# A hybrid encoder layer on one core: mLSTM scores and turned keys made once per chunk, exponent rows by DMA, query scaled ahead of its product, gates kept raw

## The reference

```
def step(carry, xs):                        # one chunk, one direction, one head
    C, n, m = carry
    qc, kc, vc, li, lf = xs
    b = cumsum(lf)
    d = b[..., :, None] - b[..., None, :] + li[..., None, :]     # lower triangle only
    m_inter = b + m
    m_t = max(m_inter, max(d))
    w_inter = exp(m_inter - m_t)
    a = (qc @ kc.T) * exp(d - m_t)
    num = w_inter * (qc @ C) + a @ vc
    den = w_inter * (qc @ n) + sum(a)
    h = num / max(|den|, exp(-m_t))
    wk = exp(g - m_new) * kc
    C_new = decay * C + wk.T @ vc ;  n_new = decay * n + sum(wk)
...
h = sigmoid(mo) * (h_fwd + h_bwd) ;  h = h * rsqrt(mean(h*h) + eps) * norm_w
merged = sigmoid(g_att) * (ya @ w_att) + sigmoid(g_mlstm) * (ym @ w_mlstm)
```

## Time and profile before

| | us |
|---|---|
| median of three runs | 2833.33 |
| span of the profiled execution | 2828.1 |
| profiled execution's own time | not listed apart; the runs lie 5.0 to 6.3 above the span |
| prologue, to the first mLSTM phase | 194.3 |
| mLSTM phase of head 1, to the turn of its values | 168.9 |
| rest of head 1 | 168.5 |
| everything behind the last attention phase | about 1243 |
| busy: PE, DVE, POOL, ACT | 2598.7, 1794.3, 1051.1, 635.4 |

### The profile page before, as it was taken

How to read it: one execution, slowest core, us unless ns; L and a number is a source line. 1 busy time by engine, 2 the same in 40 slices (tenths; PEclk the granted TensorE clock), 3 DMA queues, 4 the chain that set the end, 5 groups by cost and what they waited for, 6 DMA issues and landing times.

```text
span 2828.1 us, 40134 instructions
## 1 busy us (share of the span) xinstructions
PE 2598.7 (92%) x15036; PEld 2372.0 (84%) x15036; DVE 1794.3 (63%) x2582; ACT 635.4 (22%) x1445; POOL 1051.1 (37%) x490
## 2 busy tenths in 40 slices
PE   7799999999899989999588899898999999999996
PEld 4688778787787877788477799898999999999996
DVE  5537766687667766677767564878875126876312
ACT  4101343223431233313422101231210111111001
POOL 4511220213202221021412235565566665666663
PEclk9899999999999999999789999999999999999998
DMA  3101210112111211112242443231323233232321
GB/s 111 59 30 55 81 41 27 41 52 85 29 32 40 74 64 31 28 47 72 103 140 80 146 130 117 90 112 67 122 86 112 101 102 141 74 111 74 112 83 60
DMA packets 106845, 223.51 MB, mean 79 GB/s; under 512 B 9720, under 2 KB 52232, under 8 KB 106688
## 3 DMA queue, kind: packets, MB, share of 16 engines
q1 hardware_dynamic: 78016, 203.08, 21.0%
q10 hardware_dynamic: 28672, 18.36, 2.5%
HBM read 173.91 MB, written 47.42 MB: 78 GB/s over the span
## 4 chain that ended last, share of the span: by engine, by line
PE 72%; DVE 15%; DVEq 4%; ACT 3%; issue 3%; DMA 1%; ACTq 0%; POOL 0%; POOLq 0%; SPq 0%
PE ps L1637 18%; PE ps L1639 18%; PE ps L1638 18%; PE ps L1813 3%; PE ps L1670 2%; PE ps L1672 2%; PE ps L1671 2%; PE ps L1832 2%; DVE prob L1350 2%; DVEq L1293 1%; PE ps L1735 1%; DVE o_ld L1292 1%; PE ps L1750 1%; DVE small L1328 1%; DVE prob L1325 1%
## 5 line engine op out<-in xcount | busy, mean ns | idle before, releaser
L669 POOL TENSOR_TENSOR ring_h<-raw,colt 128x1024 fp32r<-128x1024 f32 x229 | 444.9, 1943 | 1665.3 <-PE ps L1639 948.3
L672 POOL TENSOR_TENSOR ring_l<-raw,ring_h 128x1024 fp32r<-128x1024 f32 x229 | 565.5, 2469 | 32.5
L1637 PE MATMUL ps<-ht_h,ring_h 128*128 128x512 f32 (+3 forms) x1464 | 536.1, 366 | 26.9 <-DVE ht_l L1424 9.3
L1638 PE MATMUL ps<-ht_l,ring_h 128*128 128x512 f32 (+3 forms) x1464 | 521.7, 356 | 0.0
L1639 PE MATMUL ps<-ht_h,ring_l 128*128 128x512 f32 (+3 forms) x1464 | 521.3, 356 | 0.0
L1637 PE MATMUL ps<-h_h,ring_h 128*128 128x320 f32 (+1 forms) x1408 | 440.4, 313 | 19.6 <-DVE f_z L1550 11.5
L1638 PE MATMUL ps<-h_l,ring_h 128*128 128x320 f32 (+1 forms) x1408 | 439.4, 312 | 0.0
L1639 PE MATMUL ps<-h_h,ring_l 128*128 128x320 f32 (+1 forms) x1408 | 439.2, 312 | 0.0
L1637 PEld LDWEIGHTS ps<-ht_h,ring_h 128*128 128x128 f32 x1464 | 278.6, 190 | 67.0 <-DVE ht_l L1424 10.2
L1486 DVE TENSOR_TENSOR acc<-acc,sq 128x322 f32<-128x322 f32 (+1 forms) x84 | 113.5, 1351 | 312.1 <-ACT sq L740 310.3
L1639 PEld LDWEIGHTS ps<-ht_h,ring_l 128*128 128x128 f32 x1464 | 277.9, 190 | 35.9
(11 more groups left out here) (231 smaller groups left out, 4680.1 us busy)
## 6 DMA issues: line engine op xcount, KB each, us to landing
raw<-w SPq DMA_DIRECT2D x229, 512.0 KB, 3.3
gate_scratch<-g_st SPq DMA_DIRECT2D x32, 256.0 KB, 2.0
xr<-xt SPq DMA_DIRECT2D x2, 2568.0 KB, 9.7
x_scratch<-x SPq DMA_DIRECT2D x2, 2568.0 KB, 8.6
zo_scratch<-o_st SPq DMA_DIRECT2D x40, 128.0 KB, 1.7
o_ld<-zo_scratch ACTq DMA_DIRECT2D x40, 128.0 KB, 2.1
ym_scratch<-y_st ACTq DMA_DIRECT2D x40, 128.0 KB, 1.9
ya_scratch<-ya_st ACTq DMA_DIRECT2D x40, 128.0 KB, 2.5
```

Source lines behind the costliest of these rows:

```text
L669: nc.gpsimd.tensor_tensor(ring_h[:, :, slot * P:(slot + 1) * P], raw[:, rslot], one_col.unsqueeze(2).to_broadcast([P, KT, P]), ALU.mult)
L672: nc.gpsimd.tensor_tensor(ring_l[:, :, slot * P:(slot + 1) * P], raw[:, rslot], ring_h[:, :, slot * P:(slot + 1) * P].bitcast(F32), ALU.su ...
L1637: mm(out_ap, wh, hi(k + k_first), start=first and k == 0, stop=False)
L1638: mm(out_ap, wh, lo(k + k_first), start=False, stop=False)
```

## The change

Scores and turned keys are made once per chunk, in five steps instead of ten, and ACT keeps both (the turned keys over the keys themselves). The matmuls with `pick` are gone: the exponent's row and the row of inter-chunk factors are loaded broadcast over the partitions by DMAs of ACT's queue (`load_rows`, two a step), POOL adds the mask (`mask_rows`), ACT makes the exponential with the other part as bias. POOL scales the query by its factor ahead of the product with the state (`scale_queries`, one buffer `qw`), so that both halves of the numerator add up in one bank, and it scales the keys (`scale_keys`). The two directions' updates use the same two banks, one after the other. Gates are stored raw, and their sigmoid is 0.5 (1 + tanh(z/2)), with the tanh on ACT ahead of the gate products in the last attention phase and in the mixing. Four dense groups of the mLSTM phase move: step 8 has one group, step 9 one, and three stand behind it.

On SP and POOL, and the table of dense groups:

```diff
+A_STEP = [[1]] + [[2 * i, 2 * i + 1] for i in range(1, 8)] + [[16], [17]]
...
-                    sp.wait_ge(s_g1, lin(lambda hh: 12 * hh + pos + 1, h))
+                    sp.wait_ge(ev_act, lin(lambda hh: GROUPS[("A", hh, pos)][3], h))
...
+            def mask_rows(i, h, shift=0):
+                pool.wait_ge(m_bw[i % 2], lin(lambda k: 32 * (5 * (k + shift) + i // 2 + 1), h))
+                nc.gpsimd.tensor_tensor(bw[:, i % 2, :, 0], bw[:, i % 2, :, 0], mask[:], ALU.add).then_inc(m_um, 1)
+            def scale_queries(i, h):
+                if i > 1:
+                    pool.wait_ge(m_nd, lin(lambda k: NB * k + i, h))
+                for d in range(2):
+                    if not fresh(d, i):
...
+                        last = nc.gpsimd.tensor_tensor(qw[:, d], mq_t[:, :, c * P:(c + 1) * P],
+                                                       bw[:, i % 2, d, 1].unsqueeze(1).to_broadcast([P, 2, P]),
+                                                       ALU.mult)
+                last.then_inc(m_q, 1)
+            def mlstm(h):
+                take(lambda k: a_unit(k, 0), h)
+                pool.wait_ge(m_sel, lin(lambda k: k + 1, h))
+                scale_keys(0, h)
+                take(lambda k: a_unit(k, 1), h)
+                for i in range(NB - 1):
+                    scale_queries(i + 1, h)
+                    if i + 1 < NB - 1:
+                        scale_keys(i + 1, h)
+                    if i + 2 < NB:
+                        mask_rows(i + 2, h)
+                    if i + 2 < A_UNITS:
+                        take(lambda k, u=i + 2: a_unit(k, u), h)
+            for i in range(2):
+                mask_rows(i, 0)
             with pool.Fori(0, HEADS - 1) as h:
-                for u in range(A_UNITS):
-                    take(lambda k, u=u: a_unit(k, u), h)
+                mlstm(h)
```

On ACT, the mLSTM phase:

```diff
             def mlstm(h, dense):
+                exponents(0, h)
+                keep_scores(0, h)
+                evac_a(0, h)
                 for i in range(NB):
-                    act.wait_ge(m_e, lin(lambda k: NB * k + i + 1, h))
-                    nc.scalar.activation(ex[:], ex[:], ACT.Exp).then_inc(m_x, 1)
-                    if i >= 5:
...
+                    if i + 1 < NB:
+                        exponents(i + 1, h)
+                    if i > 5:
+                        finish_y(i - 1, h)
+                    evac_a(A_STEP[i][0], h)
+                    if i + 2 < NB:
+                        load_rows(i + 2, h)
+                    if i + 1 < NB // 2:
+                        keep_scores(i + 1, h)
+                    if i >= 5:
+                        output_gate(i, h)
+                    for g in A_STEP[i][1:]:
+                        evac_a(g, h)
```

On DVE, the mLSTM phase:

```diff
+                weights(0, h)
                 for i in range(NB):
+                    normalise_h(i, h)
+                    state(0, i, h)
                     if i >= 5:
+                        gated(i, h)
+                    state(1, i, h)
                     if i + 1 < NB:
+                        weights(i + 1, h)
```

On PE, the numerator and the order of the phase, and on DVE the product with a gate:

```diff
             def m_numden(i, h):
...
+                    pe.wait_ge(m_q, lin(lambda k: 9 * k + i, h))
+                    pe.wait_ge(m_h, lin(lambda k: NB * k + i, h))
                 for d in range(2):
                     if not fresh(d, i):
+                        pe.wait_ge(m_c[d], lin(lambda k: 8 * k + updates_to(d, i - 1), h))
                         for dt in range(2):
-                            mm(ps[:, 3 + 2 * d, 0:DH + 1], mq_t[:, dt, c * P:(c + 1) * P], c_st[:, d, dt],
+                            mm(ps[:, 3 + d, 0:DH + 1], qw[:, d, dt], c_st[:, d, dt], start=dt == 0, stop=False)
...
             def mlstm(h, is_dense):
+                m_scores(0, h)
+                unit_group("A", 0, 0, h)
                 for i in range(NB):
-                    m_scores(i, h)
-                    unit_group("A", (2 * i) // 3, (2 * i) % 3, h)
                     m_numden(i, h)
+                    m_update(0, i, h)
                     if i > 5:
                         m_turn(i - 1, h)
-                    unit_group("A", (2 * i + 1) // 3, (2 * i + 1) % 3, h)
-                    m_update(i, h)
-                unit_group("A", 6, 2, h)
+                    unit_group("A", A_STEP[i][0] // 3, A_STEP[i][0] % 3, h)
+                    m_update(1, i, h)
+                    if i + 1 < NB // 2:
+                        m_scores(i + 1, h)
+                    for g in A_STEP[i][1:]:
+                        unit_group("A", g // 3, g % 3, h)
+                for g in range(18, 21):
+                    unit_group("A", g // 3, g % 3, h)
...
-                V.tensor_tensor(gw[:, a:b], gw[:, a:b], ps[:, n % 2, 0:b - a], ALU.mult).then_inc(b_mix, 1)
+                V.scalar_tensor_tensor(gw[:, a:b], gw[:, a:b], 1.0, ps[:, n % 2, 0:b - a], ALU.add, ALU.mult
+                                       ).then_inc(b_mix, 1)
```

More of the change, by code:

```diff
@@ L438, in updates, with updates_to, side @@
         return i + 1 < NB and not fresh(d, i + 1)
+    def updates_to(d, i):
+        return sum(updates(d, n) for n in range(i + 1))
+    def side(d, i):
+        return int(chunk_of(d, i) >= NB // 2)
     def tcol(q, d, h, c):
@@ L702, in _ @@
+            mlstm(HEADS - 1)
             for n in range(U_B, U_B + 2):
@@ L943, in evac_a, with exponents @@
                          rows=slice(HD, P)).then_inc(ev_act, 1)
+            def exponents(i, h):
+                act.wait_ge(m_um, lin(lambda k: NB * k + i + 1, h))
+                if i >= 2:
+                    act.wait_ge(m_nd, lin(lambda k: NB * k + i - 1, h))
+                for d in range(2):
+                    last = nc.scalar.activation(ex[i % 2][:, side(d, i)], bw[:, i % 2, d, 0], ACT.Exp,
+                                                bias=tcol(0, d, h, chunk_of(d, i)))
+                last.then_inc(m_x, 1)
@@ L1095, in attend @@
                             evac_m(g, h, 1)
+                    if not dense and j >= 1:
+                        gate_tanh(2 * j - 2)
+                        gate_tanh(2 * j - 1)
+                    if dense and j == NB - 1:
+                        act.wait_ge(a_s_done, lin(lambda k: NB * (k + 1), h))
+                        for i in range(2):
+                            load_rows(i, h, 1)
                     evac_o(j, h)
@@ L1099, in attend @@
                 store_o(NB - 1, h)
+                if not dense:
+                    for n in range(2 * NB - 2, 3 * KT):
+                        gate_tanh(n)
                 for s in range(2):
@@ new lines, in state @@
+            def state(d, i, h):
+                if not updates(d, i):
+                    return
+                dve.wait_ge(m_cu[d], lin(lambda k: 8 * k + updates_to(d, i), h))
+                src = ps[:, 5:7, 0:DH + 1]
+                if fresh(d, i):
+                    last = V.tensor_copy(c_st[:, d], src)
+                else:
+                    last = V.scalar_tensor_tensor(
+                        c_st[:, d], c_st[:, d], decay[:, bass.ds(h * NB + (d * HEADS * NB + chunk_of(d, i)), 1)], src,
+                        ALU.mult, ALU.add)
+                last.then_inc(m_c[d], 1)
@@ new lines, in normalise_h, with gated @@
+                last.then_inc(m_h, 1)
+            def gated(i, h):
+                ch = [chunk_of(d, i) for d in range(2)]
+                dve.wait_ge(m_ze, lin(lambda k: 5 * k + i - 4, h))
+                V.reciprocal(o_ld[:], o_ld[:])
+                dve.drain()
+                for d in range(2):
+                    V.tensor_tensor(h_acc[:, ch[d]], h_acc[:, ch[d]], o_ld[:, d], ALU.mult)
+                dve.drain()
+                for d in range(2):
+                    last = V.scalar_tensor_tensor(o_ld[:, d], h_acc[:, ch[d]], 1.0, h_acc[:, ch[d]],
+                                                  ALU.mult, ALU.mult, accum_out=small[:, 6 + d:7 + d])
+                last.then_inc(m_ss, 1)
@@ L1246, in mlstm @@
                     next_columns(h + 1)
+                weights(0, h)
                 for i in range(NB):
-                    step = lambda k, i=i: NB * k + i + 1
-                    ch = [chunk_of(d, i) for d in range(2)]
-                    dve.wait_ge(m_sc, lin(step, h))
-                    for d in range(2):
-                        last = V.scalar_tensor_tensor(ex[:, d], ps[:, 2, 256 * d + P:256 * d + 2 * P],
-                                                      tcol(0, d, h, ch[d]), mask[:, d], ALU.add, ALU.add)
```

274 lines of the change are left out of this document (128 added, 146 removed).

## The result

The changed kernel takes 2923.18 us (median of 4 runs, 2922.41 to 2924.74), the kernel before 2833.86 beside it: ratio 1.0317, 95% interval 1.0302 to 1.0332. It is 89 us slower, where 57 were forecast, and the median lies 1.2 us above the upper end of the range. The profiled execution took 2922.41 us, its span is 2920.6, so 92.5 above the span before. In these four runs the time lies 1.8 us above the span; by that the profile before belongs to an execution of about 2829.9 us (my estimate), 3 us under its median, and this is why the spans differ by 92.5 and the medians by 89.

The account below looks back on a forecast made before the run. PE was taken as the bound of the mLSTM phase. Per head -11.1 - 6.8 + 24.8 + 6.0 = +12.9 us; four heads +51.6, with head 0's start +57, so 2833.3 becomes 2890 us; range 2842 to 2922.

Parts of the forecast that it names:

- POOL's queue: Before step 6, PE waits for POOL's scaled query behind unit 6's split, which waits for its load: +10.4 us a head.
- The output gate's chain: Steps 6 to 8: ACT's output gate stands behind the first group's copy, so PE waits +1.9, +2.0 and +6.5 us.
- The gain on PE: mLSTM phase: ten steps of 16 passes become five of 12, at 0.111 us a pass: -11.1 us a head.
- POOL's pair of products: POOL's two query products before PE's numerator, priced from its split rows at 1.2 us with an issue between them.
- The start of head 0: POOL masks head 0's first rows before splitting unit 0, 7.5 us later with some 2 covered: +5, bounds 3 and 8.
- The other heads' starts: Row loads go out a dense group (5.5 us) earlier and unit 0 has some 5 us to spare: 0.
- Unit 5's wait: Unit 5 waits for group 8, first of step 4; the 10.4 us chain is partly covered by update and group: +4.0.
- The clock: PE runs at half clock behind the waits of 4.0, 10.4 and 6.5 us: +6.0 us a head, bounds 0 and 7.8.
- Gates: DVE's sigmoid work ends under PE's cover and the tanh moves to ACT: 0, bounds -2 and +8.
- A: POOL's queue does not hold PE, as unit loads land before step 5's end: +1.0 us a head, 2842; chance 0.10.
- B: PE stays the bound all through, as DVE is relieved in steps 5 to 9: -67 us, 2767; chance 0.06.
- C: Contention: POOL's small instructions hold each DVE chain 2 us in steps 5 to 9, 10 a head: 2930; chance 0.07.

Follow-up runs that it names:

- late_takes: Changed kernel with POOL splitting units 5 and 6 later, behind the scaled queries of steps 5 and 7: 2875.53 us, ratio 1.0146.
- the kernel start: Changed kernel with POOL splitting a head's unit 0 ahead of masking its first two row pairs: 2900.76 us, ratio 1.0239.
- the kernel three: Changed kernel with units 5 and 6 split later, ACT's output gate at the step's head and unit 0 split ahead of the first masks: 2785.58 us, ratio 0.9839.

## Why the prediction was right and where it failed

The direction and the two mechanisms were right: with POOL's queue, the output gate and the first masks put back in order, 135 us went. **POOL's queue** in front of step 6 was forecast at 10.4 us and is 11.26. **The output gate's chain** was forecast at 1.9, 2.0 and 6.5 and is 1.26, 2.09 and 6.03; the 4.5 that was to lie under unit 6's wait came up as 4.18 in late_takes. **The gain on PE** of 11.1 us a head is 8 to 10 by the doubled scores, so this term was taken 1 to 3 us a head too high. The estimate for POOL's pair of products, 1.2 us, measured 1.40; here the splits' rows were the right scale. By the GPSIMD Engine Reference (introduction) of the Trainium skill, with its factor of two, the pair would take 1.9 us (an estimate); the trace's 1.40 does not bear that out.

Span against span, the loss is 35.5 us more than forecast. The steps that failed are the starts of the heads, the landing of unit 5, and a part of the clock:

**The start of head 0, +5.** Measured: +3.8 in the prologue, and of the 28.7 of its phase 11.7 more than head 1's. The step priced the row loads and the masks (7.5 us) and took off 2 of cover, which leaves 5.5, but left out that unit 0's split stands behind them. Before the change it ran 192.16 to 196.55, beside the prologue's end. Now it follows the masks:

```profile
206.66 0.72 POOL L712 TENSOR_TENSOR bw<-bw,mask 128x256 f32<-128x256 f32 x1 [0.91 <-DMA bw<-rows_scratch]
207.34 1.89 POOL L682 TENSOR_TENSOR ring_h<-raw,colt 128x1024 fp32r<-128x1024 f32 x1
209.38 2.34 POOL L685 TENSOR_TENSOR ring_l<-raw,ring_h 128x1024 fp32r<-128x1024 f32 x1
```

PE's last score ended at 199.65. The masks ended 7.7 us behind it (207.38), where 5.5 were forecast, and the split 4.3 later: 12.1 of the 12.20 measured. The 3.8 in the prologue stay in the kernel start, and no run took them apart. I had counted what POOL's new instructions cost, and not what the old one behind them loses in cover.

**The other heads' starts, 0.** Right for heads 1 and 2, where PE has some 6.5 us of its own at the loop's end, and wrong for head 3, which is written out behind the loop and has 1.70: there the first masks ran at 1274.29 and 1276.84 and the split behind them cost 7.23 and its clock. I read one head's start and took it for all. Of the 22 us that the edit of POOL's first masks gave back, 20 lie in these two heads, against 5 forecast. With the prologue's 3.8, this one step is about half of the 35.5.

**Unit 5's wait, +4.0.** The chain was right and the landing was not: 6.85 us from issue to split in place of 3.56, as the row loads that the change adds ran beside it. The wait was 7.52, and 4.35 with them moved: 3.2 us in head 1, and 14 us over the four heads. The prediction counted the new DMAs as issues on ACT, not as traffic.

**The clock, +6.0 a head.** Head 1's account closes with 6.7 if the passes are taken at 11.1; the granted clock gives 8.7 - 1.6 = 7.1, and the fill of two waits gave 6 back. So the size was nearly right. The reading that failed is that a wait of 2.12 us leaves the clock at 1.00: of step 8's, 2.09 us long, 1.2 us were lost in head 1, and in other heads and kernels the same wait cost nothing.

**Gates, 0.** The last attention phase and mixing got 4.2 us shorter, more than the bound of -2. That was not taken apart by a run.

Of the rivals, A fell with 7.52 and 11.26 us on POOL's query, and B with 30 us of idle PE. C did not explain the changed kernel: DVE's pairs of output gate products take 0.76 to 0.82 us in all its steps and heads. But its mechanism is real. It comes up once the queues are mended: in the kernel three it is 3.4 of the 5.18 us before step 9, the largest loss left there, and in the kernel with unit 6 split last it took that wait from 6.04 to 11.59.

## What to carry to other kernels

When a critical instruction is put into the queue of an engine that waits for loads, price it at the end of the longest chain ahead of it, and price the old work behind it too: three changes of order in two queues, with no work changed, were worth 135 us and turned 3% slower into 1.6% faster. A head that is written out behind a loop starts without the loop's slack, so look at it by itself. Removing one wait lays bare the next, so the gain of a set of edits can't be added up from each alone: here it was 135 against 100.

## What the runs showed of the hardware

Idle PE costs more than its idle time: behind each wait of 7.5 and 11.3 us some 2.3 us of work were lost to the 1.2 GHz level, and filling the idle time with products that nobody reads made the kernel 25 us faster. A wait of 2.1 us cost 1.2 more in head 1 of the changed kernel and nothing in the same head of the kernel start, with long waits ahead of it in both; what decides that is open. Two broadcast loads of 128 KB each beside a 512 KB load took it from 3.67 to 6.85 us. And a DVE product of two SBUF operands was held to the end of POOL's running instruction, again and again, and took up to 4.57 us instead of 0.76; a wait that keeps POOL still for that time gained 16 us.
